# A two-layer decoder step in fp32 on one core: expert down products over whole 512-row chunks, the square-root table loaded earlier, weight units split at other places

## What is computed

```python
def _layer(x, l, ...):
    hn = rmsnorm(x, norm_mix[l])
    proj = hn @ w_in[l]                       # pooling and recurrent mixers
    ...
    x = x + mixed @ w_out[l]
    x = x + mem_attend(rmsnorm(x, norm_mem[l]), mk, mv, w_mq[l], w_mo[l])
    hn = rmsnorm(x, norm_ffn[l])
    if l % 2 == 0:
        x = x + swiglu(hn, ffn_w_gate, ffn_w_up, ffn_w_down)
    else:
        x = x + moe(hn, router_w, moe_w_gate, moe_w_up, moe_w_down)

def mem_attend(xn, k, v, wq, wo):             # 4 heads of 256, 256 memory rows
    q = (xn @ wq).reshape(B, T, 4, 256)
    p = softmax(einsum(q, k) * 256 ** -0.5)
    return einsum(p, v).reshape(B, T, 1024) @ wo

def moe(x, ...):                              # 8 experts, 2 for a token
    for e in range(8):
        out += combine[:, e:e+1] * ((silu(x @ wg[e]) * (x @ wu[e])) @ wd[e])
```

## Time and profile before

| | |
|---|---|
| runs | 1132.4, 1133.64, 1133.82 us; median 1133.64 |
| the profiled execution | 1134.49 us, of which 1132.9 us are the span of the core |
| mean granted TensorE clock | 0.967 of full |
| busy, share of the span | PE 94%, PEld 89%, DVE 69%, ACT 57%, POOL 3% |
| read from memory | 270 MB, 245 GB/s over the span |

### The profile page before, as it was taken

One profiled execution on the slowest core, in us unless ns is written; L12 is line 12 of the kernel. 1 busy time (PEld: TensorE's weight loads), 2 busy tenths in 40 slices (PEclk: granted clock), 3 DMA queues, 4 the chain that ended last, 5 costly groups with the idle time before them and its releaser, 6 DMA issues.

```text
span 1132.9 us, 19851 instructions
## 1 busy us (share of the span) xinstructions
PE 1064.1 (94%) x7638; PEld 1004.4 (89%) x7638; DVE 782.2 (69%) x1118; ACT 642.0 (57%) x858; POOL 29.4 (3%) x49
## 2 busy tenths in 40 slices
PE   4999898699999999999999698999999999999994
PEld 3999896499999999998887598999999999999993
DVE  5597643367555566698653435898898988989883
ACT  5667533355433445466533252878767776876761
POOL 0010000000000000000000001000000000000000
PEclk8999999899999999999999895999999999999997
DMA  9454469745555556554579335999989998998961
GB/s 349 149 169 143 148 240 356 307 149 175 180 184 182 178 181 186 164 164 131 162 282 361 156 102 196 359 348 361 381 312 366 361 381 293 376 333 327 345 247 41
DMA packets 65749, 278.28 MB, mean 246 GB/s; under 512 B 7512, under 2 KB 7768, under 8 KB 65024
## 3 DMA queue, kind: packets, MB, share of 16 engines
q1 hardware_dynamic: 62352, 264.33, 66.0%
q0 software_dynamic: 2880, 12.40, 3.1%
q10 hardware_dynamic: 432, 0.38, 0.1%
HBM read 270.03 MB, written 7.06 MB: 245 GB/s over the span
## 4 chain that ended last, share of the span: by engine, by line
PE 73%; DVE 14%; ACT 5%; DMA 4%; issue 3%; SPq 0%; DVEq 0%; ACTq 0%
PE bank L661 9%; PE bank L662 9%; PE bank L663 9%; PE bank L664 8%; PE bank L665 8%; PE bank L666 8%; DVE weight_lo L1542 4%; DMA ring<-dense 3%; PE bank L659 3%; PE bank L658 3%; PE bank L653 3%; ACT wh L1142 2%; DVE rstd L1537 1%; PE bank L1007 1%; DVE sq L1552 1%
## 5 line engine op out<-in xcount | busy, mean ns | idle before, releaser
L1855 DVE TENSOR_TENSOR weight_lo<-ring,wh 128x1408 fp32r<-128x1408 f32 x192 | 307.1, 1621 | 38.6 <-ACT wh L1410 35.8
L1542 DVE TENSOR_TENSOR weight_lo<-ring,wh 128x1024 fp32r<-128x1024 f32 x170 | 206.0, 1223 | 175.3 <-ACT wh L1142 174.6
L1410 ACT ACTIVATE wh<-ring 128x1408 fp32r<-128x1408 f32 x188 | 258.5, 1380 | 65.5 <-PE bank L659 54.5
L1142 ACT ACTIVATE wh<-ring 128x1024 fp32r<-128x1024 f32 x170 | 178.1, 1055 | 160.1 <-PE bank L657 132.2
L661 PE MATMUL bank<-xh,wh 128*128 128x264 f32 x812 | 238.4, 294 | 25.7 <-DVE xl L1787 12.4
L662 PE MATMUL bank<-xl,wh 128*128 128x264 f32 x812 | 234.0, 288 | 0.0
L663 PE MATMUL bank<-xh,weight_lo 128*128 128x264 f32 x812 | 233.8, 288 | 0.0
L661 PEld LDWEIGHTS bank<-xh,wh 128*128 128x128 f32 x812 | 156.5, 193 | 33.3 <-issue 15.6
L665 PE MATMUL bank<-wh,xl 128*128 128x352 f32 (+4 forms) x544 | 181.7, 334 | 0.0
L662 PEld LDWEIGHTS bank<-xl,wh 128*128 128x128 f32 x812 | 156.6, 193 | 0.1
L663 PEld LDWEIGHTS bank<-xh,weight_lo 128*128 128x128 f32 x812 | 156.1, 192 | 0.0
(11 more groups left out here) (277 smaller groups left out, 1751.5 us busy)
## 6 DMA issues: line engine op xcount, KB each, us to landing
ring<-experts SPq DMA_DIRECT2D x192, 704.0 KB, 6.1
ring<-dense SPq DMA_DIRECT2D x234, 512.0 KB, 3.7
o_k<-kv POOLq DMA_DIRECT2D x2, 1024.0 KB, 4.7
o_v<-kv POOLq DMA_DIRECT2D x2, 1024.0 KB, 8.3
x<-xT SPq DMA_DIRECT2D x2, 528.0 KB, 5.4
o_y<-sq SPq DMA_DIRECT2D x4, 264.0 KB, 2.1
gatew<-gate_w POOLq DMA_DIRECT2D x2, 512.0 KB, 8.7
mem<-memT SPq DMA_DIRECT2D x1, 1024.0 KB, 13.5
```

Source lines behind the costliest of these rows:

```text
L1142: A(high(k), raw(u), ACT.Copy).then_inc(hi_ready, 1)
L1410: A(ehigh_of(jj), eraw(jj % ESLOTS), ACT.Copy).then_inc(ehi_ready, 1)
L1542: V.tensor_tensor(low(u), raw(u), high(k).bitcast(F32), ALU.subtract).then_inc(lo_ready, 1)
L1855: V.tensor_tensor(elow_of(jj % ESLOTS), eraw(jj % ESLOTS), ehigh_of(jj).bitcast(F32), ALU.subtract).then_inc(elo_ready, 1)
```

## The change

There are four edits.

1. In the experts' down product the loop goes over the 11 chunks and no longer over the units. Before a chunk PE waits for all units in which it lies. A unit is given back with the chunk in which it ends. The transposes of the last hidden part come after chunk 2 as a whole.
2. ACT takes a square root of one column (into a buffer that is not in use) right behind the squares of `x`, ahead of the first unit's high part.
3. `upto` adds nothing for `k` up to 4. So the first norm has one unit split ahead of it, then 3 and 4 in all, where it was 3, 5 and 6.
4. In the attention, ACT splits 3 units of `mo` after its copy of chunk 2, and DVE 2 units after its low part of chunk 2; the calls behind each of the chunks 4 to 7 go. The rest follows behind chunk 7.

```diff
-            def upto(self, k):
-                k = min([k + AHEAD, NSPLIT] + [...])
+            def upto(self, k, ahead=AHEAD):
+                k = min([k + (ahead if k > 4 else 0), NSPLIT] + [...])
...
-                    for part in range(4):
-                        w_hi, w_lo = eunit(16 + 4 * u + part)
-                        f0, f1 = part * EUNIT, (part + 1) * EUNIT
-                        for kc in range(f0 // 512, (f1 - 1) // 512 + 1):
...
-                            lo, hi = max(kc * 512, f0), min((kc + 1) * 512, f1)
-                            i = product(b[:, lo - kc * 512:hi - kc * 512], ehh[:, kc, :], ehl[:, kc, :], w_hi[:, lo - f0:hi - f0],
-                                        w_lo[:, lo - f0:hi - f0], kc == 0, kc == FEC - 1, False,
-                                        last_of=eslot_free[(16 + 4 * u + part) % ESLOTS] if hi == f1 else None)
...
+                    begun, done = 0, 0
+                    for kc in range(FEC):
+                        f0, f1 = kc * 512, (kc + 1) * 512
+                        while begun * EUNIT < f1:
+                            eunit(j0 + begun)
+                            begun += 1
...
+                        over = (done + 1) * EUNIT <= f1
+                        i = product(b[:, :], ehh[:, kc, :], ehl[:, kc, :], w_hi[:, f0:f1], w_lo[:, f0:f1], kc == 0, kc == FEC - 1, False,
+                                    last_of=eslot_free[(j0 + done) % ESLOTS] if over else None)
...
+                        done += over
+                        if u == 0 and over and done == 1:
                             turn_hidden(num, 3)
...
                 if l == 0:
+                    step(A(rms[:, 1, 0:1], eps[:, 0:1], ACT.Sqrt))
                     S.upto(start("in", l) + 1)
...
                     A(xhi[:, m, 0:TP], bank(n)[:, 0:TP], ACT.Copy).then_inc(oh_ready, 1)
-                    if m >= 4:
-                        S.upto(start("mo", l) + m - 3)
+                    if m == 2:
+                        S.upto(start("mo", l) + 3, 0)
...
                 for m in range(3):
                     prompt_low(m)
+                S.upto(start("mo", l) + 2, 0)
...
                 for m in range(4, KC):
                     prompt_low(m)
-                    S.upto(start("mo", l) + m - 3)
+                S.upto(start("mo", l) + 4)
```

More of the change, by code:

```diff
@@ L550, in __init__ @@
                 self.at, self.one = 0, one
-            def upto(self, k):
-                k = min([k + AHEAD, NSPLIT] + [max(k, split[("mo", l, 0)]) for l in range(DEPTH) if k <= split[("mo", l, 0)]])
+            def upto(self, k, ahead=AHEAD):
+                k = min([k + (ahead if k > 4 else 0), NSPLIT] + [max(k, split[("mo", l, 0)]) for l in range(DEPTH) if k <= split[("mo", l, 0)]])
                 while self.at < k:
@@ L1061, in expert @@
                     b = take_bank(n, more)
-                    for part in range(4):
-                        w_hi, w_lo = eunit(16 + 4 * u + part)
-                        f0, f1 = part * EUNIT, (part + 1) * EUNIT
-                        for kc in range(f0 // 512, (f1 - 1) // 512 + 1):
[L1066 to L1069, removed]
-                            lo, hi = max(kc * 512, f0), min((kc + 1) * 512, f1)
-                            i = product(b[:, lo - kc * 512:hi - kc * 512], ehh[:, kc, :], ehl[:, kc, :], w_hi[:, lo - f0:hi - f0],
-                                        w_lo[:, lo - f0:hi - f0], kc == 0, kc == FEC - 1, False,
-                                        last_of=eslot_free[(16 + 4 * u + part) % ESLOTS] if hi == f1 else None)
-                        if part == 3:
+                    j0 = 16 + 4 * u
+                    w_hi = wh[:, 0:4 * EUNIT]
+                    w_lo = weight_lo[:, j0 % ESLOTS * EUNIT:(j0 % ESLOTS + 4) * EUNIT]
+                    begun, done = 0, 0
[4 more added lines that the diff above has]
+                            begun += 1
+                        if u == 0:
+                            for i4, (c0, c1) in enumerate(TURNS):
+                                if kc == c0:
+                                    wait_read(pe, *num(f"T{i4}"))
+                        over = (done + 1) * EUNIT <= f1
+                        i = product(b[:, :], ehh[:, kc, :], ehl[:, kc, :], w_hi[:, f0:f1], w_lo[:, f0:f1], kc == 0, kc == FEC - 1, False,
+                                    last_of=eslot_free[(j0 + done) % ESLOTS] if over else None)
+                        if kc == FEC - 1:
                             full(i, n)
-                        else:
+                        elif over:
                             i.then_inc(eunit_used, 1)
-                        if u + part == 0:
+                        done += over
+                        if u == 0 and over and done == 1:
                             turn_hidden(num, 3)
```

## The result

The changed kernel takes 1116.95 us (median of 4 runs, 1113.92 to 1120.69) against 1133.02 for the kernel before in the same series: a ratio of 0.9865 (95% interval 0.9843 to 0.9887), that is 16.1 us less. A second series gave 1117.72 us (5 runs) and a ratio of 0.9844 (0.9819 to 0.9869). The forecast was 1117.

The account below looks back on a forecast made before the run. PE, busy for 94% of the span, was taken as the bound. Start 3.4, attention 6.7 and experts 6.8 sum to 16.9 us off the profiled 1134.49, 1117.6; the median lies 0.85 lower, so 1117, range 1112 to 1124.

Parts of the forecast that it names:

- The start, forecast 3.4: First norm: early table load and fewer units split ahead let the root begin 3.4 us earlier, all reaching the end.
- the root then begins at 12.95: First norm on ACT: the root follows PE's sums directly, at 12.95 us in place of 16.40.
- stall for its fifth unit: First projection: a stall there for the fifth unit would show the prediction wrong; without cover it would lose 1 us.
- Edit 4, the waits, forecast 5.7: Attention's end: output projection starts earlier by 2.1 us in layer 0 and 3.6 in layer 1, together 5.7.
- the wait ahead of the projection was to fall to 1.4: Attention's end: PE's wait ahead of the output projection falls from 6.1 us to about 1.4.
- the new one was to be over 3 us: Attention's end: a new PE wait of over 3 us ahead of `prompt_values(3)`, as the copy into `o8` comes later.
- Edit 4, the clock, forecast 1.0: Attention's end: one 3.2 us low-clock stretch per layer, 1.6 us each, remains within chunks or projection; 1.0 us comes back.
- A second stretch behind the new gap: Attention's end: a second stretch at granted clock 0.50 following the new gap would show the prediction wrong.
- Edit 1, forecast 6.8: Experts' down product: whole chunks take both banks from 16.38 to 15.53 us, 0.85 an expert, 6.8 for 8 experts.
- no wait of PE for `weight_lo`: Experts: PE never waits for low parts; more than 0.1 us a chunk would show the prediction wrong.
- slower rival: Experts: 48 chunks wait for a second unit; beyond 0.35 us each the change loses, 1141 at 0.5; chance 0.02.
- The rival in which a cut costs some ns: Experts' down product: a cut costs only its fixed part, so the experts keep their time; 1123 us, chance 0.02.

Follow-up runs that it names:

- edit 2 alone: Kernel before plus only the early one-column square root behind the squares of `x`; 1130.89 us, ratio 0.9986.
- edit 4: As a profiled run: kernel before plus only the `mo` units split ahead of chunk 3 at the attention's end; 1127.24 us, ratio 0.9936.
- gap filled: Kernel before plus 20 fp32 matmuls of 128 columns that nothing reads, ahead of each layer's attention output projection; 1131.86 us, ratio 0.9973.
- edit 1 alone: Kernel before plus only the loop over whole chunks in the experts' down product; 1124.74 us, ratio 0.9931.
- edits 2 and 3 alone: Kernel before plus only the early square root and one unit split ahead of the first norm; 1129.32 us, ratio 0.9961.
- the old cuts put back: Changed kernel with down-product chunks 2, 5 and 8 cut as before (384+128, 256+256, 128+384), waits and transposes as changed; 1125.11 us, ratio 0.9920.
- last kernel: Changed kernel without the early square root, and with DVE's copy into `o8` ahead of its two `mo` units; 1110.79 us, ratio 0.9798.

## Why the prediction was right, point by point

**The start, forecast 3.4.** Right in size, and wrong in whose merit it is. In the profiles the first product is at 19.76 to 20.32 with the old start (19.26 with edit 2 alone) and at 16.06 to 17.48 with the new one. It scatters more now, as the root hangs on PE's sums: these took from 5.29 to 6.82 us for the same 16 matmuls. Means of 20.0 (four profiles: before, edit 1, edit 4, gap filled) and 17.0 (the nine with edit 3) give 3.0 us. The step "the root then begins at 12.95" held (12.60, with the sums 0.49 earlier). But I booked the two edits as one. Edit 3 does it all but for at most 0.2 us, and edit 2 by itself moves the wait to DVE. The first projection did not stall for its fifth unit.

**Edit 4, the waits, forecast 5.7.** Right step by step in the first profile. The copy was to come 4.8 us behind L837's start and came 4.68 behind; the wait ahead of the projection was to fall to 1.4 and fell to 1.60 and 1.72; the new one was to be over 3 us and is 3.24. The stages lost 1.9 and 3.5 us against 2.1 and 3.6 forecast. But the 3.6 of layer 1 owes something to luck. It rests on a fourth `sample_values` of 3.49 us there, which delays the copy by itself, so that DVE's two units cost less on top; the profile of before and the first one of after both happen to have it. Add up PE's two waits of a layer, ahead of the fourth chunk and ahead of the projection. With the old tail they are 6.8 to 7.0 us in all ten cases. With edit 4 they are 4.8 to 5.0 in the eight cases with a `sample_values` of 1.91 us and 3.0 to 3.4 in the four with a slow one. So the waits give 2 us in a layer or 3.7, in the mean 5.2 for both layers together.

**Edit 4, the clock, forecast 1.0.** The assumption was one stretch of low clock for each layer, now within the chunks or the projection. The first profile has one such stretch in the two layers together (L837 in layer 1, 3.49 us), and none behind the new wait. The second one has it in both layers, over the chunks (5.22 us in layer 0, 5.39 in layer 1). So the term is not one number. Nor did it stay within the assumption: in layer 1 of the second profile the granted clock is 0.50 for 6.8 us (624.3 to 631.1) and the chunks take 2.7 us longer, where 1.6 was assumed. A second stretch behind the new gap was one of the forecast's own signs of being wrong, and here it came. Over all kernels the whole of edit 4 comes to 7.3 where 6.7 were forecast, within the scatter; taking off the 5.2 of the waits leaves 2.1 for the clock in place of 1.0.

**Edit 1, forecast 6.8.** Each expert's banks lost 0.88 us, 7.1 in all, and edit 1 alone had 6.84 of them in the whole experts. Handed back: 0.3 us in that profile. In the changed kernel's first profile more seems lost (5.23), but 1.4 of the difference to its second (6.65) is low clock at the experts' begin. The forecast "no wait of PE for `weight_lo`" was slightly off: 0.7 us in two waits, 0.3 in one in the second profile. They don't come from the new loop, as edit 1 alone has none and the old loop has some too (edits 2 and 3 alone). Nothing comes near the 0.35 us a chunk of the slower rival.

**The rival in which a cut costs some ns.** By measurement a chunk's three matmuls cost 0.05 us more when cut in halves, and 0.20 with a piece of 128 columns; putting all cuts back cost 7.4 us. The earlier trace rows were right. The Trainium skill, "TensorE: Matmul & The Clock Gate", section "Back-to-back issue gap", gives 2.5 ns beside the columns for a lone matmul, from which I had estimated 0.4 us for all. The same section of the Trainium skill says of this formula that in a real stream it counts too little for narrow matmuls. The trace agrees with that, with 0.11 us where the columns alone take 0.06, so the formula was not to be taken for a rival's price here. Why the second and the third narrow matmul take 0.11 us was not isolated. Each matmul has a weight load of its own, and behind the first narrow one the loads begin 0.11 us apart as well (at 784.23, 784.34, 784.45 and 784.56 with the old cuts put back). No kernel here took the loads away.

**The sum.** By terms as measured it is 3.0 + 7.3 + 6.8 = 17.1 us; by time it is 16.1 and, in the second series, 17.7 (0.9844 of 1133). The single edits' ratios add up to 0.69 + 0.39 + 0.64 = 1.72%, or 19.5 us, each with an error of about 0.2%, so that a loss through their meeting is not shown. That the median hit the forecast to 0.1 us is luck: each term is known to a us or two, and the executions of one kernel spread over 7 us.

## What to carry over

A wait that is moved has to be priced on both engines. Edit 4 emptied one queue ahead of the projection and put 2.7 us ahead of a copy for which PE stood still; the forecast had this number in it, and moving one call behind that copy gives another 5 to 8 us. In a stream of matmuls look at the distance of the starts by width before cutting: here a piece of 128 columns cost about as much as one of 256, so cuts should fall into halves or not be made. And before adding an early table load, see whether the engine has idle time where the load would land by itself.

## What the runs showed of the hardware

- The same 16 sums at the start took 5.29 to 6.82 us in different executions, and the fourth `sample_values` 1.91 or about 3.5 us; the long ones of the latter lie in stretches at a granted clock near 0.5 (0.52 in the earlier trace rows's execution and with the gap filled, 0.54 with edits 2 and 3 alone). They follow waits of 1.78 to 2.08 us, but others of 1.8 to 2.0 us had none: of 28 cases 9 were slow (one of them 2.76 us at 0.67). In five of nine profiles with the new start both were long (sums 6.57 to 6.82, `sample_values` of layer 0 3.37 to 3.58) and in the other four neither was. What ties them is open.
- In the 28 layers of these 14 profiles: behind PE's waits of 6.1 to 6.4 us the low level came in ten cases of ten. Behind those of 3.2 us ahead of the fourth value chunk it came in six of eight. Behind those of 1.4 to 1.8 us ahead of the projection it came in none of eighteen. Behind one of 0.59 us (last kernel, layer 1) the chunks were slow too, 2.07 us for 1.13, but there the matmuls ahead of it had been slow already (2.76 us for 1.91).
- Some 4.6 us of matmuls that nothing reads, put into a gap of 6, kept the level at 1.00 behind it in both layers (one execution).
- At the 2.4 GHz level matmuls with a weight load each start 0.23 us apart at 512 columns, 0.18 at 384, 0.12 at 256, and 0.11 at 128 but for the first behind a wider one, which takes 0.06. The first whole matmul behind narrow ones takes 0.29.
- A square-root table load took 1.28 us and did not wait for its ACTIVATE's input: it ran from 11.08 to 12.36, the input came at 13.54.
